# The first two experts' rows picked on TensorE as whole token rows, and the last place of the expert loop given to a sorted expert of 64 rows

## The reference, cut to what matters

```python
def _hier_moe(h, p):
    gl = (h @ p['w_group_router']).astype(jnp.float32)
    g_sel = jax.nn.one_hot(jnp.argmax(gl, axis=-1), N_GROUPS, dtype=jnp.float32)
...
    top_v, top_i = lax.top_k(el_sel, TOP_K)
    top_w = jax.nn.softmax(top_v, axis=-1) * g_p[..., None]
...
        a = jnp.einsum('bsd,edf->bsef', h, p['w_e1'][gi])
        b = jnp.einsum('bsd,edf->bsef', h, p['w_e3'][gi])
        y = y + jnp.einsum('bsef,efd->bsd', jax.nn.silu(a) * b * w_all[:, :, gi, :, None], p['w_e2'][gi])
```

## Time and profile before

| | us |
|---|---|
| median of 3 runs | 1884.13 |
| the profiled execution's own time | 1894.46 |
| its span, first to last instruction | 1892.7 |
| TensorE busy | 1782.1 (94%) |
| VectorE busy | 813.7 (43%) |
| ScalarE busy | 442.7 (23%) |
| GpSimd busy | 122.4 (6%) |
| HBM read | 386.38 MB |

### The profile page before, as it was taken

The page is one execution under the profiler, slowest core; times in us unless marked ns, Lnnn a source line. Parts: engine busy times, 40 slices in busy tenths (PEclk is TensorE's granted clock), DMA queues, the critical chain, the costliest instruction groups (busy, mean ns, idle before and its releaser), DMA issues.

```text
span 1892.7 us, 25310 instructions
## 1 busy us (share of the span) xinstructions
PE 1782.1 (94%) x10202; PEld 1095.7 (58%) x10202; DVE 813.7 (43%) x1850; ACT 442.7 (23%) x956; POOL 122.4 (6%) x160
## 2 busy tenths in 40 slices
PE   6999999999999989997789999999999998999887
PEld 3445656688777773332245565667888877333223
DVE  1295473565544451111133966536655455111113
ACT  3312344333100121010043134334321112111002
POOL 0001201000000030000020020010000003000002
PEclk9999999999999989998989999999999998999988
DMA  9662293413556658999952221323123335899994
GB/s 403 224 261 91 95 361 106 156 68 112 198 221 270 245 200 353 425 427 426 424 209 101 110 94 58 131 93 120 69 90 112 133 151 201 326 424 425 428 427 156
DMA packets 51926, 422.42 MB, mean 223 GB/s; under 512 B 6448, under 2 KB 7872, under 8 KB 28768
## 3 DMA queue, kind: packets, MB, share of 16 engines
q1 hardware_dynamic: 33696, 369.35, 48.9%
q0 software_dynamic: 9632, 33.07, 5.1%
q10 hardware_dynamic: 8480, 18.35, 2.6%
HBM read 386.38 MB, written 32.28 MB: 221 GB/s over the span
## 4 chain that ended last, share of the span: by engine, by line
PE 81%; DMA 14%; another core or an unknown queue 1%; issue 1%; DVE 1%; ACT 1%; SPq 0%; POOL 0%; ACTq 0%; DVEq 0%
PE psum L871 19%; PE psum L1148 19%; PE psum L1137 9%; PE psum L1319 8%; PE psum L874 7%; DMA pc<-we_in 6%; DMA ring<-we_in 6%; PE psum L1340 2%; PE psum L791 2%; PE psum L1324 2%; DMA ring<-wch_in 2%; PE psum L849 1%; PE psum L1223 1%; PE psum L1335 1%
## 5 line engine op out<-in xcount | busy, mean ns | idle before, releaser
L871 PE MATMUL psum<-hT,ring 128*128 128x384 f32 x1088 | 363.9, 489 | 0.1
L871 PEld LDWEIGHTS psum<-hT,ring 128*128 128x128 f32 x1088 | 202.9, 190 | 141.2 <-issue 12.4
L1137 PE MATMUL psum<-pc,ring 128*128 128x384 f32 x512 | 175.6, 486 | 0.0
L1319 PE MATMUL psum<-ring,scr 128*64 128x512 f32 x512 | 126.9, 653 | 30.9 <-DMA ring<-we_in 27.1
L2625 DVE TENSOR_TENSOR ytok<-pc,psum 128x256 f32<-128x256 f32 (+1 forms) x32 | 15.1, 471 | 323.1 <-ACT pc L1815 323.1
L1148 PE MATMUL psum<-hT,ring 128*128 128x192 f32 x768 | 143.0, 329 | 1.8 <-ACT vals L1514 1.8
L1148 PEld LDWEIGHTS psum<-hT,ring 128*128 128x128 f32 x768 | 126.1, 190 | 18.6 <-issue 9.6
L1319 PE MATMUL psum<-pc,scr 128*64 128x512 f32 x512 | 118.0, 615 | 18.7 <-DMA pc<-we_in 18.7
L2015 DVE SCALAR_TENSOR_TENSOR pc<-pc,par 128x384 f32<-128x384 f32 x240 | 127.2, 605 | 0.0
L874 PE MATMUL psum<-ring,hT 128*128 128x512 f32 x288 | 125.2, 593 | 0.0
L1137 PEld LDWEIGHTS psum<-pc,ring 128*128 128x128 f32 x512 | 94.4, 190 | 51.9
(11 more groups left out here) (421 smaller groups left out, 2383.8 us busy)
## 6 DMA issues: line engine op xcount, KB each, us to landing
ring<-we_in SPq DMA_DIRECT2D x48, 2048.0 KB, 17.8
pc<-we_in SPq DMA_DIRECT2D x48, 2048.0 KB, 20.0
ring<-wch_in SPq DMA_DIRECT2D x18, 2048.0 KB, 8.3
ring<-wgate_in SPq DMA_DIRECT2D x16, 2048.0 KB, 8.4
ring<-wmod_in SPq DMA_DIRECT2D x18, 1024.0 KB, 6.7
pc<-wmod_in SPq DMA_DIRECT2D x24, 768.0 KB, 7.7
ring<-wbr_in SPq DMA_DIRECT2D x16, 1024.0 KB, 4.8
ring<-wtok_in SPq DMA_DIRECT2D x6, 2048.0 KB, 8.9
```

What stands on the lines that cost most here:

```text
L871: mm = pe.matmul(F[:, 0:T], wv[:, k, n * P:(n + 1) * P], hT[:, k, :], start=k == 0, stop=k == KD - 1)
L1137: mm = pe.matmul(bank(7)[:, 0:T], wv[:, c, (n % 4) * P:(n % 4 + 1) * P], pc[:, MERGE_SLOT[i], c, :], start=c == 0, stop=c == 3)
L1319: mm = pe.matmul(bank(2)[BIG * h:BIG * h + BIG, :], x_h[:, k, 0:BIG], w[h][:, k, :], start=k == 0, stop=k == KD - 1, skip_group_check=True)
```

## The change

**Picking.** Places 0 and 1 are both picked on TensorE, with the operands exchanged: the 0/1 matrix is stationary (64 columns, then 32) and the token rows move (512 or 256 channels at a time). The result is rows, in the layout of a loaded tile. So it is copied to SBUF (place 0 by ScalarE, place 1 by VectorE), turned by the same `turn_rows` as every other place and copied to `x_h`. Place 1's rows are no longer loaded from DRAM.

**The last place.** `FREE` now runs to expert 15: 14 experts are sorted, and the one with the fewest tokens comes last, 64 rows wide. Its `project` is one part in two column halves (L1341) instead of two parts of 96 rows. VectorE finds out which expert it is (`last_one`) with some more small operations.

```diff
-FREE = range(2, NE - 1)
+FREE = range(2, NE)
...
-RANK_AT = (3, 4, 0, 5, 1, 6, 2, 7, 8, 9, 10, 11, 12)
+RANK_AT = (3, 4, 0, 5, 1, 6, 2, 7, 8, 9, 10, 11, 12, 13)
...
# TensorE
                 def turn_rows(e):
-                    pe.wait_ge(rows_in[e % 2].sem, rows_in[e % 2].at(l, rows_loaded(e)))
+                    if e == 1:
+                        pe.wait_ge(pick_ready.sem, pick_ready.at(l, 4))
+                    elif e > 1:
+                        pe.wait_ge(rows_in[e % 2].sem, rows_in[e % 2].at(l, rows_loaded(e)))
                     for b, pieces in ((0, 4), (1, 2)) if wide(e) else ((0, 4),):
+                        if e == 0:
+                            pe.wait_ge(ht_copied.sem, ht_copied.at(l, 7 + b))
...
-                        if e == NE - 1:
-                            mm = pe.matmul(bank(5 + n)[0:CAP, :], x_gT[:, f, :], w2[:, f, n * 512:(n + 1) * 512],
-                                           start=f == 0, stop=f == 3)
-                            continue
...
                 pe.wait_ge(ht_copied.sem, ht_copied.at(l, 6))
-                pe.wait_ge(pick_ready.sem, pick_ready.at(l, 1))
-                for k in range(KD):
-                    for t in range(NT):
-                        mm = pe.matmul(x_turned[:, k, :], htok[:, t, k * P:(k + 1) * P], first_pick[:, t * P:t * P + CAP],
-                                       start=t == 0, stop=t == NT - 1, skip_group_check=True)
-                mm.then_inc(xt_done.sem, 1)
+                for e in range(2):
+                    pe.wait_ge(pick_ready.sem, pick_ready.at(l, e + 1))
+                    for b, size, lo, width in ((0, BIG, 0, 512), (1, SUB, BIG, 256)):
+                        for t in range(NT):
+                            one = first_picks[e][:, t * P + lo:t * P + lo + size]
+                            for c in range(P // size):
+                                mm = pe.matmul(bank(4 * e + b)[size * c:size * c + size, 0:width], one,
+                                               htok[:, t, c * width:(c + 1) * width], start=t == 0, stop=t == NT - 1,
+                                               skip_group_check=True)
+                    mm.then_inc(xt_done.sem, 1)
+                turn_rows(0)
...
+                project(NE - 1, 0)
                 for t in range(2):
-                    project(NE - 1, t)
# ScalarE
-                    if e == 0:
-                        ac.activation(x_h, x_turned, ACT.Copy).then_inc(xh_ready.sem, 1)
-                        return
...
+                ac.wait_ge(xt_done.sem, xt_done.at(l, 1))
+                for b, picked_rows in enumerate(x_rows[0]):
+                    ac.activation(picked_rows, bank(b)[:, 0:512 // (b + 1)], ACT.Copy).then_inc(ht_copied.sem, 1)
                 copy_rows(0)
...
-                load_rows(1)
                 load_rows(2)
...
-                for n in range(2):
-                    keep_last(n)
+                ac.wait_ge(xy_done.sem, xy_done.at(l, parts_to(NE)))
+                for c in range(2):
+                    ac.activation(x_last[:, c * W:(c + 1) * W], bank(5)[BIG * c:BIG * c + BIG, :], ACT.Copy)\
+                      .then_inc(xy_ready.sem, 1)
# VectorE
-                for t in range(NT):
-                    o = ve.tensor_scalar(first_pick[:, tok(t)], cc("iota"), rk[:, t, 0:1], None, ALU.is_equal)
-                o.then_inc(pick_ready.sem, 1)
+                for e in range(2):
+                    for t in range(NT):
+                        o = ve.tensor_scalar(first_picks[e][:, t * P:t * P + CAP], cc("iota", 0, CAP), rk[:, t, e:e + 1], None,
+                                             ALU.is_equal)
+                    o.then_inc(pick_ready.sem, 1)
...
-                step(ve.memset(rmul[:, :, NE - 1:NE], 1.0))
+                step(ve.tensor_scalar(last_one[:, 0, FREE.start:FREE.stop], rank, float(RANK_AT[-1]), None, ALU.is_equal))
+                chain.settle()
+                of_last = last_one[:, :, :].to_broadcast([P, NT, NE])
+                step(ve.tensor_tensor(rmul[:, :, :], rmul[:, :, :], of_last, ALU.max))
...
+                for of, to in ((rk, v1), (rw, v2)):
+                    step(ve.tensor_tensor(sel[:, :, :], of[:, :, :], of_last, ALU.mult))
+                    chain.settle()
+                    step(ve.tensor_reduce(to, sel[:, :, :], AX.X, ALU.add))
+                    chain.settle()
...
                 ve.tensor_copy(slot_back[:, :], rt[:, 146:152]).then_inc(slot_ready.sem, 1)
+                ve.wait_ge(xt_done.sem, xt_done.at(l, 2))
+                for b, picked_rows in enumerate(x_rows[1]):
+                    o = ve.tensor_copy(picked_rows, bank(4 + b)[:, 0:512 // (b + 1)])
+                o.then_inc(pick_ready.sem, 1)
```

More of the change, by code:

```diff
@@ L193, in rows_loaded @@
 def rows_loaded(i):
-    return sum(32 if wide(j) else 16 for j in range(1, i + 1) if j % 2 == i % 2)
+    return sum(32 if wide(j) else 16 for j in range(2, i + 1) if j % 2 == i % 2)
 CTX, LAT = slice(0, SEQ), slice(SEQ, T)
@@ L279, in hybrid_step @@
         sort_pair = sb("sort_pairs", [P, NF_SORT, NF_SORT])
+        last_one = sb("last_expert", [P, 1, NE])
         sort_count = sb("sort_count", [1, NE])
@@ L540, in hybrid_step @@
         ht_done = sig("ht_done", 6)
-        ht_copied = sig("ht_and_last_pick_copied", 7)
+        ht_copied = sig("ht_first_rows_and_last_pick_copied", 9)
         rows_zeroed = sig("expert_rows_zeroed", 0)
         slot_ready = sig("slots_order_and_slots_back_ready", 3)
-        pick_ready = sig("expert_picks_ready", 2)
+        pick_ready = sig("expert_picks_and_second_rows_ready", 4)
         scattered = sig("rows_scattered", 2 * NT * 16)
         rows_in = [sig(f"expert_rows{i}_in", rows_loaded(NE - 2 + i)) for i in range(2)]
-        xt_done = sig("rows_turned", NE)
+        xt_done = sig("rows_picked_or_turned", NE + 2)
         xh_ready = sig("rows_turned_ready", NE)
@@ L1370, in _ @@
                     if e == 0:
-                        pe.wait_ge(pick_ready.sem, pick_ready.at(l, 2))
+                        pe.wait_ge(pick_ready.sem, pick_ready.at(l, 3))
                         for t in range(NT):
@@ L1377, in _ @@
                 hidden(NE - 1)
-                pe.wait_ge(ht_copied.sem, ht_copied.at(l, 7))
+                pe.wait_ge(ht_copied.sem, ht_copied.at(l, 9))
                 pe.wait_ge(spill_known.sem, spill_known.at(l, 1))
@@ L1421, in _ @@
                 for n in range(KD):
-                    pe.wait_ge(xy_ready.sem, xy_ready.at(l, parts_to(NE) - 1 + n // 4))
+                    pe.wait_ge(xy_ready.sem, xy_ready.at(l, parts_to(NE - 1) + 1 + n // 4))
                     for t in range(0 if n >= KD - 2 else 2, NT):
                         turn_back(n, t)
-                    pe.matmul(back_bank(n)[:, 0:T], x_last[:, n * P:(n + 1) * P], last_pickT[0:CAP, :], start=False, stop=True,
+                    pe.matmul(back_bank(n)[:, 0:T], x_last[:, n * P:(n + 1) * P], last_pickT[0:BIG, :], start=False, stop=True,
                               skip_group_check=True).then_inc(out_done.sem, 1)
@@ L1875, in _ @@
             ve.memset(room32[:, :], float(CAP - BIG))
+            ve.memset(last_one[:, :, :], 0.0)
             ve.memset(small[:, 60:62], 0.0).then_inc(setup_s.sem, 1)
@@ L2602, in _ @@
                     slots = rt[:, 146 + 3 * k:149 + 3 * k].rearrange("p (t a) -> p t a", t=NT)
-                    step(ve.tensor_scalar(gden, one_of[k][:, :, NE - 1:NE], 0.0, None, ALU.is_equal))
+                    step(ve.tensor_tensor(sel[:, :, :], one_of[k][:, :, :], of_last, ALU.mult))
+                    chain.settle()
+                    step(ve.tensor_reduce(gden, sel[:, :, :], AX.X, ALU.add))
+                    chain.settle()
+                    step(ve.tensor_scalar(gden, gden, 0.0, None, ALU.is_equal))
                     chain.settle()
@@ L2793, in _ @@
                         gp.indirect_dma_start(
-                            to, None, ys_d[0:(NE - 1) * CAP, :], bass.IndirectOffsetOnAxis(slot_back[:, k * NT + t:k * NT + t + 1], 0),
-                            bounds_check=(NE - 1) * CAP - 1, oob_is_err=False).then_inc(back_in[t].sem, 16)
+                            to, None, ys_d, bass.IndirectOffsetOnAxis(slot_back[:, k * NT + t:k * NT + t + 1], 0),
+                            bounds_check=NE * CAP - 1, oob_is_err=False).then_inc(back_in[t].sem, 16)
                 for n in range(1, 1 + POOL_SQUARES):
```

21 lines of the change are left out of this document (9 added, 12 removed).

## The result

| | before | after |
|---|---|---|
| median of the paired runs, us | 1883.36 (1882.15 to 1886.51, 4 runs) | 1909.43 (1907.33 to 1913.76, 4 runs) |
| ratio after / before, 95% interval | | 1.0139 [1.0117, 1.0161] |
| the profiled execution, us | 1894.46 | 1910.19 |
| its span and mean granted clock | 1892.7, 0.972 | 1908.3, 0.969 |

The change makes the kernel 26 us slower. The two profiled executions lie only 15.7 us apart, because that of before was itself 10.3 us above its median.

A forecast was written before the change was run, and what follows sets the result against it. Each layer's expert stage was taken as bound by a full DMA weight stream between a head and a gather-ended tail. Terms 2.2 + 0.6 - 0.6 - 3.6 - 3.1 + 1.9 = -2.6 us took 1884.13 to 1881.5, range 1876 to 1887.5.

The forecast's parts named there:

- the tail: Expert stage's end, up to L1425: gathers end it, the fifth and sixth go out earlier; -3.6 us layer 0, -3.1 layer 1.
- a low clock in the last loop: Final loop on TensorE: named among the signs that would show the forecast wrong; no size given.
- clock again: New TensorE waits before `hidden(0)` and L1425, both layers: one low-clock spell of 3.8 us charged, +1.9 (bounds 0 and 7.6).
- my 4.03 us a place: Picks in the head: 6 matmuls at 2.66 plus 12 at 1.37 us per place, at full clock.
- The head: Picks up to `hidden(0)`: both places take 8.06 us at full clock, plus low-clock loss; +2.2 us layer 0, +0.6 layer 1.
- Rival two: Ahead of `hidden(0)`, both layers: picks run at the lower clock throughout; +8.8 us in all, 1892.9; chance 0.08.
- The stream: Expert weights between head and tail: as long as its bytes, one load 128 KB less; 0.3 us a layer, -0.6.
- rival three: Tail: gathers land no earlier, transfers always the limit or ScalarE held elsewhere; +4.1 us, 1888.2; chance 0.09.
- Nothing in the change scales with that: Whole kernel: the profiled execution's 10.3 us above the median stays constant, so median 1884.13 becomes 1881.5 us.

The follow-up runs named there:

- the usual before: The kernel before, unedited, in its second profile (experiment 1): span 1879.2 us, clock 0.982.
- experiment 3: Kernel before with the last place's sums over 64 partitions, rows 64 to 95 left out: ratio 1.0077 to the kernel before.
- experiment 8: Changed kernel, sums over 64 partitions, with 7, 5 and 4 throwaway matmuls in the waits for the gathers: ratio 1.0113 to the kernel before.
- experiment 7: Changed kernel with sums over 96 partitions and 7, 5 and 4 throwaway matmuls in the waits for the gathers: ratio 1.0083 to the kernel before.
- experiment 9: Changed kernel with sums over 96 partitions and 3, 2 and 2 throwaway matmuls in the waits: ratio 1.0027 to the kernel before.
- experiment 10: Changed kernel, sums over 64 partitions, with 3, 2 and 2 throwaway matmuls in the waits: ratio 1.0074 to the kernel before.
- experiment 2: Changed kernel with the last place's sums over 96 partitions again, 32 with zero weights: ratio 1.0060 to the kernel before.
- experiment 6: Kernel before with only the last-place half of the change, sums over 96 partitions: ratio 1.0020 to the kernel before.
- experiment 1: The kernel before, no edit, profiled once more: 1880.94 us in its one run.

## Why the prediction was wrong

I forecast 1881.5 us (1876.0 to 1887.5); it is 1909.4.

- **The step that failed: the final loop was never priced.** The part on the tail ends at the start of L1425 and counts nothing behind it. But the change makes `x_last` 64 rows high, and with it the contraction of the final sums. That price is +9.9 us in each loop and some 2 behind it, 24 of the 29 us against the usual before. It has two halves, shown apart. The changes of height cost 8.97 - 6.40 = 2.6 us a loop at full clock (experiments 3, 8). The low clock costs the other 7.3 (8.97 to 16.29). I had named "a low clock in the last loop" as what would make me wrong, and priced **clock again** at +1.9 for one spell of 3.8 us; the runs showed spells of 27 us in each layer.
- **Where the low clock comes from.** Two things together. TensorE waits 2.77, 1.95 and 1.87 us ahead of the loop since it has no second half of `project(15)` any more; with filled waits the clock was 1.00 up to the loop in experiments 7 to 9 and in layer 0 of experiment 10. And the changed kernel's loops over 64 partitions, which start at 0.50, stay there to their end (16.3 us), where those over 96 have 1.00 back in their third to fifth step (experiments 2, 6); only in layer 1 of experiment 10 did a loop over 64 that began low have it back, after 0.3 us. The waits I had foreseen, and charged too little for. Why the clock stayed down over 64 partitions these runs don't show. The waits alone don't decide it: layer 1 of experiment 3 lost the clock one step into its loop, and none of the loops over 72 or 96 partitions that began at full clock did.
- **A price that one pair of rows seemed to rule out.** TensorE's new list changes between 64, 32 and 128 columns five times where the old one changed none. I weighed that for the picks alone, where columns change, from one pair of rows: L1324 (32 columns) starts at 711.56, right where L1319 (64 columns) ends, so I charged nothing. I had set a start against an end, and the profile models the ends. The starts of single instructions show a price there too: in the picks of place 1, matmuls of 64 columns start in pairs 0.43 us apart, and the first of 32 columns start 0.53 behind the last pair (701.72 to 702.25). In all it is 0.12 us for a change from 64 to 32 columns and 0.17 for one from 32 to 64 or to 128. That is some 0.6 us of each head, of which my 4.03 us a place held a part: from start to start a place took 4.16. For rows it is 0.17 us a change as well, between 64 and 128; 72 and 96 partitions beside 128 showed none (a step of 0.75 and 0.76 us), and why 64 does the runs don't show.
- **The head: mechanism right, size off.** I said +2.2 and +0.6. Over all profiles it is +3.3 and +2.6. Against the usual before it was +5.1 in layer 0. The spells of low clock in my sum, 6.6, 3.3 and 3.8 us long, are the three windows of the earlier trace rows, granted 0.50, 0.50 and 0.55. I had compared the new picks at a mixed clock with old ones that ran at half clock for 6.6 of 8.8 us; at full clock on both sides it is 10.15 against 6.47. Rival two, picks at low clock throughout, was in no profile: the first place's picks took up to 7.13 us, but the second place's ran at full clock (1.00) each time. The two longest heads (experiments 9 and 10) hold pauses besides.
- **The stream** was -0.6 for both layers in the sum, and -1.1 and -0.5 in the traces. DMA share 1.01 over the same 206 us, as said.
- **The tail: right as a difference to that trace, but the gain wasn't there.** ScalarE's third scaling came 13.6 us behind the first gather, against 13 forecast and 15.5 before; from `hidden(15)` to the first sum the tail fell by 3.2 and 2.3 us, against 3.6 and 3.1. But the usual before has that scaling at 13.7 us too, and tails of 22.6 / 22.8. Against it the tails gave +0.6 us in all where the sum has -6.7, the second largest miss. Letting the fifth gather go 1.8 us sooner behind the first (5.3 instead of 7.1 us, layer 0) brought the last rows 0.1 us sooner. So rival three, gathers that land no earlier, describes the usual before; that the transfers were the limit there is argued, not shown.
- **"Nothing in the change scales with that."** So I carried the profiled execution's 10.3 us over the median along as a constant. They lay in the very stages that the change touches: mostly low-clock spells (0.50 over 6.6 and 3.3 us of the picks), and in the tails `turn_hidden(15)` waited 2.71 us for VectorE where the usual before has 1.20. A trace so far above its median isn't a neutral base; the gains I read from it were in part a recovery that most executions have without any change.

## What to carry to other kernels

Price every matmul whose operand changes its shape, also those that the diff touches only through the size of a tile; between neighbours over 128 partitions, don't let a contraction fall to 64 (0.34 us a step at full clock here); with zero weights over 96 partitions the price is gone (0.76 us a step, 0.75 with 72). Before removing work from an engine that waits, see what clock the next dense stretch starts with: here, with 3.6 us of "hidden" matmuls in one of the waits, the loop behind them ran at 1.00 and took 6.4 us (experiment 1), and without them it began at 0.50 and took 8.4 to 9.5 (experiments 2, 6). And compare with a second profile of the kernel before when the first lies well above its median.

## What the runs showed of the hardware that was not expected

- A matmul (two instructions) over 64 partitions between transposes over 128: 1.10 us a step instead of 0.76 at full clock, 1.98 instead of 1.49 at half. Side by side, at half clock, 0.66 an instruction. With 72 partitions 0.75 a step.
- Changes of the columns cost alike, at full clock: 0.12 us from 64 to 32, 0.17 from 32 to 64 or 128.
- With about the same waits ahead of it (3.18, 1.88 and 1.27 us against 2.77, 1.95 and 1.87 in layer 0), a dense loop of 96-partition steps got the full clock back 4.4 us into it, and one of 64-partition steps did not in 16 us. In one layer of experiment 3 such a loop lost it after a single step; in the other, and in the four loops behind filled waits, it kept it, save for a tenth of a microsecond of loop time in one.
- The same 48 instructions of the old picks took 5.57 us in one execution and 8.82 in another, by whether a low spell fell on them: a granted clock of 1.00 over all of them in the one, of 0.50 for 6.6 us in the other.
